# Two pairs of gathers handled together at every second slot, one gelu for four dots, in a single-core transformer block with a 16,384-expert retrieval layer

## The reference, cut to what matters

```python
u = expert_u[idx]                      # 128 rows of 1024 for each token
v = expert_v[idx]
act = jax.nn.gelu(jnp.einsum('thkd,td->thk', u, xb), approximate=False)
return jnp.einsum('thk,thkd->td', (g * act).astype(xb.dtype), v)
```

## Time and profile before

| | us |
|---|---|
| median of three runs | 3633.49 |
| profiled execution, its own time | 3634.84 |
| its span in the profile | 3633.0 |
| TensorE busy (matmul) | 2843.4 (78%) |
| VectorE busy | 2214.6 (61%) |
| ScalarE busy | 690.8 (19%) |
| GpSimd busy | 1154.4 (32%) |
| gather queue (software_dynamic) | 1078.00 MB, 72.3% of 16 DMA engines' span |
| weights and the rest (hardware_dynamic) | 224.01 MB, 16.8% |

### The profile page before, as it was taken

How to read it: one execution, slowest core, us unless ns; L and a number is a source line. 1 busy time by engine, 2 the same in 40 slices (tenths; PEclk the granted TensorE clock), 3 DMA queues, 4 the chain that set the end, 5 groups by cost and what they waited for, 6 DMA issues and landing times. The chain is left out here.

```text
span 3633.0 us, 31949 instructions
## 1 busy us (share of the span) xinstructions
PE 2843.4 (78%) x11208; PEld 1447.6 (40%) x11208; DVE 2214.6 (61%) x5619; ACT 690.8 (19%) x1255; POOL 1154.4 (32%) x1036
## 2 busy tenths in 40 slices
PE   8889867899987857799988867798988835555555
PEld 3568632355645413355645322345653501111111
DVE  1231277875554886875554887775554787666665
ACT  2230113621111113622111112531111000000000
POOL 0000013433332333433332233343332334444442
PEclk9999988899998978999998878899998968777777
DMA  5324559999999999999999999999999959999998
GB/s 166 107 93 151 174 194 408 393 423 409 418 425 371 401 387 361 391 386 409 418 425 374 386 398 369 369 367 412 418 425 410 414 227 399 427 427 421 427 427 350
DMA packets 212016, 1304.05 MB, mean 359 GB/s; under 512 B 25216, under 2 KB 25744, under 8 KB 80272
## 3 DMA queue, kind: packets, MB, share of 16 engines
q0 software_dynamic: 148608, 1078.00, 72.3%
q1 hardware_dynamic: 63248, 224.01, 16.8%
HBM read 1288.28 MB, written 13.63 MB: 358 GB/s over the span
## 5 line engine op out<-in xcount | busy, mean ns | idle before, releaser
L626 POOL DMA_INDIRECT rowbuf<-in_peer_uv,idx x884 | 987.7, 1117 | 2204.8 <-PE acc L923 1522.6
L923 PE MATMUL acc<-rowbuf,diag 128*64 128x512 f32 x3536 | 1069.4, 703 | 406.0 <-DVE diag L1602 397.7
L1592 DVE CUSTOM_DVE_ANT_0 rowbuf<-rowbuf,xr 128x1024 f32<-128x1024 f32 x884 | 1058.2, 1220 | 273.3 <-DMA rowbuf<-in_peer_uv,idx 269.5
L923 PEld LDWEIGHTS acc<-rowbuf,diag 128*64 128x64 f32 x3536 | 260.4, 154 | 1023.1 <-DVE diag L1602 530.1
L1192 ACT ACTIVATE acts<-dots 128x2 f32<-128x2 f32 x512 | 104.1, 203 | 2249.3 <-DVE dots L1592 2175.5
L1602 DVE TENSOR_SCALAR diag<-consts,acts,gw 128x64 f32<-128x64 f32 x1024 | 287.8, 344 | 291.4 <-ACT acts L1192 122.8
L675 PE MATMUL bank<-xnT,W 128*128 128x256 f32 x1600 | 366.8, 385 | 0.0
L675 PEld LDWEIGHTS bank<-xnT,W 128*128 128x128 f32 x1600 | 300.5, 191 | 87.3 <-issue 48.7
L661 PE MATMUL bank<-W,xnT 128*128 128x512 f32 x736 | 334.1, 604 | 0.5 <-ACT kv L978 0.5
L675 PE MATMUL bank<-arena,W 128*128 128x256 f32 x1024 | 245.4, 398 | 57.5 <-DMA W<-in_w_blocks 56.4
L923 PE MATMUL acc<-kv,diag 128*64 128x512 f32 x440 | 192.9, 758 | 90.4 <-DVE diag L1602 86.7
(11 more groups left out here) (190 smaller groups left out, 2394.2 us busy)
## 6 DMA issues: line engine op xcount, KB each, us to landing
W<-in_w_blocks SPq DMA_DIRECT2D x360, 512.0 KB
rowbuf<-in_peer_uv,idx POOLq DMA_INDIRECT x884
xs<-in_x SPq DMA_DIRECT2D x16, 512.0 KB
xr<-x SPq DMA_DIRECT2D x32, 256.0 KB
out_y<-xs SPq DMA_DIRECT2D x8, 512.0 KB
x<-arena SPq DMA_DIRECT2D x8, 512.0 KB
out_y<-xr POOLq DMA_DIRECT2D x8, 512.0 KB
xs<-memory SPq DMA_DIRECT2D x3, 1024.0 KB, 8.9
```

Source lines behind the costliest of these rows:

```text
L626: pool.indirect_dma_start(rows[SLOT[g]], None, a["peer_uv"], bass.IndirectOffsetOnAxis(ap=idx[:, at // NB, at % NB:at % NB + 1], axis=0)). ...
L923: mm = pe.matmul(acc[HP * j:HP * (j + 1), h * HALF:(h + 1) * HALF], diag[:, c % DIAGS, j, :], v[:, D + h * HALF:D + (h + 1) * HALF], start ...
L1592: dve.tensor_tensor_reduce(out=u, in0=u, in1=xr[:, t, j, :], scale=1.0, scalar=0.0, op0=ALU.mult, op1=ALU.add, accum_out=dots[:, c % QS, j ...
```

## The change

Slots are left where they are, but the odd ones do nothing. At an even slot c VectorE now weighs c and c+1 and then takes the four dots of c+2 and c+3; ScalarE makes one gelu of four dots (of c+2 and c+3); TensorE adds c-2 and c-1. `begin` takes the dots of the first two picks, `catch_up` adds the last two, `finish` of the first tile moves from slot 65 to slot 66 of the step. A fourth diagonal buffer is added. ScalarE waits for `route_done` before it copies the gate projection ("GG"), whose room the ranking still uses.

```diff
--- before.py
+++ after.py
@@ -206,7 +206,7 @@
 
 NB = HEADS * TOPK
 PAIRS = NB // 2
-DIAGS, QS = 3, 4
+DIAGS, QS = 4, 4
 ROWS = 11
 KV_ROWS, KV_UNTIL = 4, 184
 EXTRA = W_SLOTS // 2 + KV_ROWS
@@ -926,11 +926,13 @@
 
             def slot(c):
 
-                if c % (NT * PAIRS):
+                if c % 2 == 0 and c % (NT * PAIRS):
+                    add(c - 2)
                     add(c - 1)
 
             def catch_up(n):
 
+                add(NT * PAIRS * n - 2)
                 add(NT * PAIRS * n - 1)
 
             picks = Picks(slot)
@@ -1035,6 +1037,8 @@
                 if n == 1:
                     norm_heads(norm_no("XQ", n), ("XQ", n), view(("XQ", n), 1024), filled(("XQ", n)), 8, XA_D)
                 picks.upto(("GG", n))
+                if n > 1:
+                    act.wait_ge(route_done, NT * (n - 1))
                 act.wait_ge(*filled(("GG", n)))
                 act.activation(ggT, view(("GG", n), T)[0:GL_R, :], ACT.Copy).then_inc(free_sem(("GG", n)), 1)
                 picks.upto(("GL", n))
@@ -1188,12 +1192,13 @@
                 act.activation(bf[:, 4, :, :].rearrange("p a b -> p (a b)"), bf[:, 4, :, :].rearrange("p a b -> p (a b)"), ACT.Exp).then_inc(sm_exp, 1)
 
             def gelu(c):
-                act.wait_ge(dot_done, 2 * c + 2)
-                act.activation(acts[:, c % QS, :], dots[:, c % QS, :], ACT.Gelu).then_inc(gelu_done, 1)
+                act.wait_ge(dot_done, 2 * c + 4)
+                act.activation(acts[:, c % QS:c % QS + 2, :].rearrange("p a b -> p (a b)"), dots[:, c % QS:c % QS + 2, :].rearrange("p a b -> p (a b)"),
+                               ACT.Gelu).then_inc(gelu_done, 1)
 
             def slot(c):
-                if (c + 1) % (NT * PAIRS):
-                    gelu(c + 1)
+                if c % 2 == 0 and (c + 2) % (NT * PAIRS):
+                    gelu(c + 2)
 
             picks = Picks(slot)
             for n in range(STEPS + 1):
@@ -1594,7 +1599,7 @@
 
             def weigh(c):
 
-                dve.wait_ge(gelu_done, c + 1)
+                dve.wait_ge(gelu_done, c // 2 + 1)
                 if c >= DIAGS:
                     dve.wait_ge(rows_added, c - DIAGS + 1)
                 at = 2 * (c % PAIRS)
@@ -1607,16 +1612,21 @@
 
                 dve.wait_ge(xr_in[0], 64 * n)
                 dot(NT * PAIRS * (n - 1))
+                dot(NT * PAIRS * (n - 1) + 1)
 
             def slot(c):
                 n, rel = c // (NT * PAIRS) + 1, c % (NT * PAIRS)
-                if rel == PAIRS + 1:
+                if rel % 2:
+                    return
+                if rel == PAIRS + 2:
                     finish(n, 0)
                 weigh(c)
-                if rel + 1 == PAIRS:
+                weigh(c + 1)
+                if rel + 2 == PAIRS:
                     dve.wait_ge(xr_in[1], 64 * n)
-                if rel + 1 < NT * PAIRS:
-                    dot(c + 1)
+                if rel + 2 < NT * PAIRS:
+                    dot(c + 2)
+                    dot(c + 3)
 
             def finish(n, t):
                 g = NT * (n - 1) + t
```

## The result

The changed kernel takes 3842.8 us (median of four runs, 3840.98 to 3854.49) against 3633.72 us for the kernel before in the same comparison: 209 us more, ratio 1.0588, 95% interval [1.0576, 1.0601]. The forecast was +22 us, to 3655.5 us, with a range of 3608 to 3705 us. The direction was forecast; the size is nearly ten times the forecast's.

A forecast was written before the change was run, and what follows sets the result against it. The prediction took the kernel to wait for DMA most of the time. Its terms, 13 - 8 + 8 + 6 + 3 = +22 us on 3633.5 us, gave 3655.5 us, with a range of 3608 to 3705 us.

The forecast's parts named there:

- the tight case: Picks 220 to 383, 82 pairs with 11 buffers, where a gather's buffer release and its dot meet in slot c-2.
- (a): Attention of step 4, 11 buffers: 20 us of stalls in 14 pairs, 7 us gained from table loads; +13 us.
- (b): Attention of steps 2 and 3, 13 and 12 buffers: no stall, table-load saving capped by idle DMA; -8 us.
- the count above: Slots from a buffer's add to the next dot: with 12 buffers, pick c-5 is added two slots earlier, so no stall.
- (c): The other 68 pairs with 11 buffers: stalls mostly hidden by full DMA; +8 us, bounds -10 and +95.
- the 11-buffer meeting of add and dot: With 11 buffers, TensorE adds pick c-4 in the slot where VectorE wants the dot; 1.4 us stall a pair.
- the 72 us of idle VectorE: Projection stretches, 2550 to 2700: VectorE busy 78 of 150 us, so stalls there were to cost nothing.
- The third rival: Ring too short everywhere with 11 buffers, 80 us for 23 pairs: 3727 us, half as bad 3690; chance 0.16.
- (d): Entry to the ranking of step 4: MAX8 8.5 us late, 2.8 us of pick work already done; +6 us.
- (e): End of the run: last gelu leads to four diagonals and 16 matmul records in place of 8; +3 us.
- Put at nothing: Second dot in `begin`, fourth diagonal buffer, ScalarE's wait for `route_done`, `finish` at slot 66: claimed to cost nothing.

The follow-up runs named there:

- e6: Kernel before with gathers of u alone, v rows left out, TensorE adding u times x, all instructions and waits kept: 3325.4 us, ratio 0.9156.
- e2: Kernel before, picks one by one, with dot and gelu one slot earlier (those of c+2 in slot c): 3674.8 us, ratio 1.0125.
- e5: Changed kernel with TensorE adding one pick in every slot and the four dots and their gelu moved to the odd slot: 3658.8 us, ratio 1.0094.
- e10: e2 with one gelu for two picks at every odd slot: 3651.4 us, ratio 1.0054.
- e12: Kernel before with TensorE's add one slot later (c-2 in slot c) and a fourth diagonal buffer: 3630.3 us, ratio 1.0019.
- e13: Kernel before with the changes of e2 and e12 together, nothing in pairs: 3732.3 us, ratio 1.0298.
- e1: Changed kernel with TensorE adding one pick in every slot, as before: 3768.4 us, ratio 1.0383.
- e3: Changed kernel with its four dots and their gelu moved to the odd slot behind: 3728.7 us, ratio 1.0274.

## Why the prediction was wrong

**What bounds the kernel.** This premise failed first. I read DMA shares of 0.94 to 1.00 as "the kernel waits for DMA", and so took a stall for a wait on engines that are full anyway. In e6 the three steps still take 96% of their time with half the bytes in every gather. That the change "can only fill idle DMA time or make more of it" made stalls outside the tight case look free; in truth time that VectorE spends waiting for a row can go on top of the chain of the engines' work.

**(a) Attention of step 4**, +13 us forecast. From the first to the last of the maxima it took 102 us (2282 to 2384) and takes 122 (2429 to 2551): +20 us. The forecast was for a longer stretch, the 28 picks from 2250 to 2420: from the gelu of slot 268 to that of slot 296 it took 171 us (2245.54 to 2416.17) and takes 215 (2375.14 to 2589.82), +44 us, with VectorE waiting 41.0 us for rows and a DMA share of 0.72. The forecast mechanism, rows that are late for a dot in the chain, stands in the slot shown above. Its size was forecast at less than a third, and what four dots in one go hold up on ScalarE was put at nothing ("The gelu waits half as often for twice as long: nothing").

**(b) Attention of steps 2 and 3**, -8 us forecast. 79 to 87 us and 87 to 102 us from first to last maxima: +24 us. The step that failed is "no stall by the count above": I counted only whether the last gather's buffer was free two slots earlier, not whether the row had also come through the queue by then. In step 3 e2 has a least distance of two slots and loses 25 us.

**(c) Everything else in steps 1 to 3**, +8 us forecast, bounds -10 and +95. Here lies most of it: 205 - 20 - 24 = 161 us outside the maxima of the three attentions, with (d). Taken wider, from the transposes (L686) ahead of an attention to the next projection (L661) on TensorE, the attentions lose 16, 25 and 32 us, and 132 us are left. So this term, put at +8, is the one that was most in error. The bound was drawn from 68 pairs in the stretch with 11 buffers; steps 1 and 2 lose 55 and 72 us too. The forecast had itself named the test: if steps 1 and 2 lose as much as step 3, "the reason is not the 11-buffer meeting of add and dot". They lose 55 and 72 us against 78, so that meeting is not the reason for most of it. That "its cover is the 72 us of idle VectorE" did not hold; that this idle time is VectorE waiting in the same chain, so that late work is handed on, fits the slot above but was not tested by itself. The third rival (the ring too short everywhere with 11 buffers) had the right sign with 3690 to 3727 us, missed the loss with 13 and 12 buffers, and was too low by more than half; its 3.5 us a pair was applied to 23 pairs.

**(d) Ranking of step 4**, +6 us forecast. From its first MAX8 to the first gather of step 4, 130 us before (2840.86 to 2970.65) and 128 after (3045.54 to 3173.23): no loss.

**(e) The end**, +3 us forecast. The last pick of the changed kernel:

```profile
3824.59 1.22 DVE L1597 CUSTOM_DVE_ANT_0 kv<-kv,xr 128x1024 f32<-128x1024 f32 x1 [1.24 <-DMA kv<-in_peer_uv,idx]
...
3832.31 1.22 DVE L1634 COPY xr<-acc 128x1024 f32<-128x1024 f32 x1 [5.24 <-PE acc L923]
```

7.72 us from last dot to copy, 4.08 in the earlier trace rows: +3.6 us. Right.

**Put at nothing.** The second dot in `begin`, the fourth diagonal buffer and ScalarE's wait for `route_done` are all in e5 too, whose steps 1 and 2 are 2 us shorter and 1 us longer than before. No loss of theirs shows there, though the paired gelu in e5 may hide a few us.

**The gelu.** "Half the gelus mean half the table loads": the gelu's group falls from 100 loads to 84, as only 100 of 512 gelus had a load before; the others followed one another with the table in place. In the attention it is 17 for 28 gelus, and 13 for 15 now (2350 to 2580). What the paired gelu is worth all the same, 24 us, showed only in e10 against e2. The 1.28 us of a load stayed 1.28 us, and the next instruction follows at once: a load at 2429.34, its exponential at 2430.64.

**The distance in slots**, 3 before and 0 after for the last gather with 11 buffers, was counted rightly and then priced from one row, in which TensorE led by 1.8 us and nothing was in the queue. The price of the distances between was not looked at. The runs give 46 us for one slot taken by earlier dots (e2), 5 us for one taken by later adds (e12), and 107 us for both (e13).

## What to carry to other kernels

In a ring of buffers that engines pass round in a fixed order of slots, count the slots between producer and consumer for every hand-over, the one from the release of a buffer to its next use too. The sum is fixed by the number of buffers, and work in pairs takes from it at both ends, as rows are wanted earlier and buffers come back later. The count warns of a loss but does not give its size. The one gain of fewer, larger instructions measured here is 24 us (e10 against e2), and no version with them beat the kernel before. A DMA share near one doesn't show that DMA sets the time: halve the bytes and look.

## What the runs showed that I had not expected

With half the bytes in every gather the three steps became 3.5% shorter at a DMA share of 0.71 (e6), while the last step, which has nothing beside it, went from 662 to 439 us. VectorE's wait for rows is no measure of the loss by itself: `rowbuf` waits of 448.5 us cost 5 us in e12, and 553.0 us cost 46 us in e2:

```profile
DVE rowbuf L1596 <- DMA rowbuf<-in_peer_uv,idx: 553.0, 373, 6.0
```

Open is how the 102 us of pairing divide between four rows wanted at once, four buffers back at once, and the longer hold on ScalarE; e1 says 69 us for the adds in pairs, e3 109 us for where the dots stand, and they overlap.
